# Banks of product tiles handed out by age across products; VectorE adds a group's first bank ahead of its split

## What is computed

```python
# block 1
r, k, v = (x_r @ w_r, x_k @ w_k, x_v @ w_v)       # 2048 x 2048 each
y = recurrence(r, k, v, ...) @ w_o                # 2048 x 2048
x = x + gate * rms(y)
u = causal_dwconv(norm(x) @ ffn_w_in)             # 2048 x 11008
f = (silu(gate_half(u)) * value_half(u)) @ ffn_w_out   # 5504 x 2048
x = x + gate * rms(f)
# block 2
p = rms(x) @ w_in_2                               # 2048 x 5376
x = x + rms(concat(attention(p), hgrn2(p)) @ w_out_2)  # 2048 x 2048
h = rms(x) @ w_up_2                               # 2048 x 8192
x = x + rms(relu(h)**2 @ w_down_2)                # 8192 x 2048
```

## Time and profile before

| | us |
|---|---|
| runs of the kernel before | 3032.55, 3021.90, 3033.14 |
| their median | 3032.55 |
| the profiled execution | 3020.16 |
| its span in the profile | 3018.2 |

### The profile page before, as it was taken

One profiled execution on the slowest core, in us unless ns is written; L12 is line 12 of the kernel. 1 busy time (PEld: TensorE's weight loads), 2 busy tenths in 40 slices (PEclk: granted clock), 3 DMA queues, 4 the chain that ended last, 5 costly groups with the idle time before them and its releaser, 6 DMA issues.

```text
span 3018.2 us, 45825 instructions
## 1 busy us (share of the span) xinstructions
PE 2813.4 (93%) x19618; PEld 2380.1 (79%) x19618; DVE 1869.0 (62%) x2460; ACT 1283.6 (43%) x1735; POOL 100.8 (3%) x127
## 2 busy tenths in 40 slices
PE   6999986898988899999989999999999999999997
PEld 2487875777877688788878878888978888888886
DVE  3776745676655577657757656566657556566554
ACT  1243423333214655445425545456555444343443
POOL 0101101111000000000000000000000000000000
PEclk9999997898889999999999999999999999999999
DMA  9766642232216266666665554443444555555552
GB/s 380 252 237 205 209 167 67 85 111 78 79 64 212 95 226 193 223 212 207 224 194 182 183 180 131 165 145 106 132 146 165 192 186 187 173 191 182 169 194 84
DMA packets 289212, 514.11 MB, mean 170 GB/s; under 512 B 10097, under 2 KB 122737, under 8 KB 288881
## 3 DMA queue, kind: packets, MB, share of 16 engines
q1 hardware_dynamic: 286016, 500.21, 49.4%
q0 software_dynamic: 2560, 7.90, 0.8%
q10 hardware_dynamic: 432, 3.07, 0.3%
HBM read 508.91 MB, written 2.10 MB: 169 GB/s over the span
## 4 chain that ended last, share of the span: by engine, by line
PE 81%; DVE 8%; ACT 5%; issue 3%; DMA 2%; POOL 0%; DVEq 0%; SPq 0%; ACTq 0%
PE ps L767 43%; PE ps L769 21%; PE ps L733 2%; PE ps L906 1%; DMA RAWa<-in_ada_w 1%; PE ps L901 1%; DVE WLb L1702 1%; ACT WHb L1195 1%; PE ps L676 1%; PE ps L891 1%; PE ps L794 1%; PE ps L868 1%; PE ps L858 1%; PE ps L788 1%; PE ps L957 1%
## 5 line engine op out<-in xcount | busy, mean ns | idle before, releaser
L767 PE MATMUL ps<-XB,WHb 128*128 128x512 f32 x2304 | 831.6, 404 | 30.1 <-DVE WLb L1702 19.2
L769 PE MATMUL ps<-XB,WLb 128*128 128x256 f32 x2304 | 646.8, 281 | 0.0
L1702 DVE TENSOR_TENSOR WLb<-RAWb,WHb 128x2048 fp32r<-128x2048 f32 (+1 forms) x196 | 426.2, 2191 | 315.5 <-ACT WHb L1195 315.3
L767 PEld LDWEIGHTS ps<-XB,WHb 128*128 128x128 f32 x2304 | 437.4, 190 | 138.2 <-issue 24.5
L1702 DVE TENSOR_TENSOR WLd<-RAWd,WHd 128x2048 fp32r<-128x2048 f32 x144 | 328.6, 2290 | 325.6 <-ACT WHd L1195 325.6
L1195 ACT ACTIVATE WHb<-RAWb 128x2048 fp32r<-128x2048 f32 (+1 forms) x196 | 356.8, 1832 | 332.4 <-PE ps L769 330.5
L767 PE MATMUL ps<-XD,WHd 128*128 128x512 f32 x1280 | 461.9, 403 | 4.1 <-DVE R L1754 3.2
L769 PEld LDWEIGHTS ps<-XB,WLb 128*128 128x128 f32 x2304 | 439.3, 191 | 1.2
L1195 ACT ACTIVATE WHd<-RAWd 128x2048 fp32r<-128x2048 f32 x144 | 274.8, 1915 | 364.9 <-PE ps L769 364.9
L767 PE MATMUL ps<-FB,WHd 128*128 128x512 f32 x1024 | 364.8, 400 | 2.7 <-DVE UM L2309 2.7
L769 PE MATMUL ps<-XD,WLd 128*128 128x256 f32 x1280 | 361.0, 282 | 0.0
(11 more groups left out here) (329 smaller groups left out, 3518.6 us busy)
## 6 DMA issues: line engine op xcount, KB each, us to landing
RAWb<-in_ffn_w_in SPq DMA_DIRECT2D x168, 512.0 KB, 5.1
RAWd<-in_w_up SPq DMA_DIRECT2D x64, 1024.0 KB, 5.2
RAWd<-in_w_down SPq DMA_DIRECT2D x64, 1024.0 KB, 5.1
RAWa<-in_ada_w SPq DMA_DIRECT2D x48, 1024.0 KB, 7.4
RAWa<-in_rwkv_w_rkv SPq DMA_DIRECT2D x48, 1024.0 KB, 5.8
RAWb<-in_ffn_w_out SPq DMA_DIRECT2D x36, 1024.0 KB, 5.2
RAWs<-in_ada_w SPq DMA_DIRECT2D x32, 1024.0 KB, 5.1
RAWb<-in_w_in SPq DMA_DIRECT2D x44, 512.0 KB, 4.8
```

The source lines that it names most:

```text
L767: pe.matmul(bank[:, :], WH[tag][:, w, o:o + P], acts(k), start=(k == 0), stop=False)
L769: mm = pe.matmul(bank[:, 0:T], WL[tag][:, w, o:o + P], acts(k)[:, 0:T], start=False, stop=last)
L1702: dve.tensor_tensor(WL[tag][:, n % WN, 0:size], RAW[tag][:, slot, 0:size], WH[tag][:, n % WN, 0:size].bitcast(F32), ALU.subtract).then_inc ...
```

## The change

Two edits. The banks are handed out from a list in order of age: a tile takes the bank that has been handed out longest ago (among the first five in `g_r`, the first six in `g_p`), and the list goes on from product to product. It begins again at banks 0 to 6 in order at `g_r`, `g_o`, the first product of `g_f`, `g_p` and `g_o2`. And in the products that accumulate, VectorE adds the first tile of a group ahead of `walk`, so ahead of the split of chunk n + 2, and the other tiles behind it as before. ScalarE's and TensorE's code stay as they are, apart from the bank numbers.

```diff
         tile_bank, tile_before, in_bank = [], [], {}
+        by_age = []
         for gm in [g_r, g_k, g_v, g_o] + [x for p in g_f for x in p] + [g_p, g_o2] + [x for p in g_m for x in p]:
+            if gm in (g_r, g_o, g_f[0][0], g_p, g_o2):
+                by_age = list(range(7))
             for i in range(gm.tile0, gm.tile_end):
-                b = (i - gm.tile0) % {g_p: 6, g_r: 5}.get(gm, 7)
+                b = next(b for b in by_age if b < {g_p: 6, g_r: 5}.get(gm, 7))
+                by_age.remove(b)
+                by_age.append(b)
                 tile_bank.append(b)
                 tile_before.append(in_bank.get(b))
                 in_bank[b] = i
@@ vector_program: gemm
                         last = ch is chunks[-1]
+                        if last and evac is accumulate:
+                            accumulate(gm, g, 0, 1)
                         if last and g in evac_first:
                             evac(gm, g)
                         walk(min(ch["number"] + 2, limit - 1))
                         if hook:
                             hook(g, ci)
-                        if last and g not in evac_first:
+                        if last and evac is accumulate:
+                            accumulate(gm, g, 1, n_tiles(gm, g))
+                        elif last and g not in evac_first:
                             evac(gm, g)
@@
-            def accumulate(gm, g):
-                for t in range(n_tiles(gm, g)):
+            def accumulate(gm, g, first, end):
+                for t in range(first, end):
                     i, d = gm.base[g] + t, to_r(gm, g, t)
                     dve.wait_ge(s_tile, i + 1)
                     dve.tensor_tensor(d, banks[tile_bank[i]][:, 0:T], d, ALU.add).then_inc(s_acc, 1)
```

## The result

| | us |
|---|---|
| changed kernel, four runs | 2991.95, 2983.63, 2987.64, 2987.84 |
| its median | 2987.74 |
| kernel before, four runs | 3032.55, 3021.90, 3033.14, 3018.68, median 3027.23 |
| ratio | 0.9872, 95% interval 0.9839 to 0.9904 |
| spans of the profiled executions, before and after | 3018.2 and 2990.0 |

The change makes the kernel 1.3% faster. The forecast was a gain of 32.1 us, subtracted from a median of 3032.55, which with more runs turned out to be 3027.2. The forecast time of 3000.5 is 12.8 us above the measured median. Of these, 5.3 us are the base that was too high, and 7.4 us are gain: the medians of this set lie 39.5 us apart, 7.4 more than forecast.

A forecast was written before the change was run, and what follows sets the result against it. TensorE, busy 93% of the span, was taken to lose time to bank waits and its lower clock; 2.1 + 1.7 + 13.8 + 6.6 + 6.3 + 1.9 - 0.3 = 32.1 us off 3032.55 gave 3000.5, range 2984 to 3013.

The forecast's parts named there:

- 18 bank waits: At product starts and groups' fourth tiles, 31.7 us together: 16 were to go, those in g_k and g_v to shrink.
- 13.8 + 6.6 us: Ten waits at product starts gone, 13.8 us; six at fourth tiles in two short-chunk products gone, 6.6 us.
- 2.1 + 1.7 us: Waits at the starts of g_k and g_v shrink to 3.97 and 3.56 us, moving to the fourth tile.
- The restart: TensorE's slower first matmuls after a wait: 0.12 us at each of 16 waits, 1.9 us gained.
- The second chunk of a product, costed at nothing: After the restart in g_k, the second chunk's split was to end well ahead of its turn, costing nothing.
- The clock: Lower clock behind three waits goes with them, 6.3 us gained; the falls in g_k and g_v were left in.
- the clock rival: The clock stays up in g_k and g_v too: 4.7 us more gain, 2996 us, chance 20%.
- Edit 2 outside the short chunks: VectorE's early first tile brings nothing in g_m, and the later split is costed at nothing in mid-product.
- cover: In accumulating groups the moved split of chunk n + 2 still ends 3.4 us before TensorE needs the chunk.

The follow-up runs named there:

- both_again: The changed kernel run once more with no edit: median 2992.23 us of four runs, ratio 0.9891 to the kernel before.
- banks_by_age_alone: The changed kernel without VectorE's early first tile, only the list by age: median 3003.18 us, ratio 0.9925 to the kernel before.
- all_tiles_ahead: The changed kernel, but VectorE adds all four tiles of an accumulating group ahead of the split: median 2988.42 us, ratio 0.9879 to the kernel before.
- split_done_twice: all_tiles_ahead with the split behind an accumulating group made twice, same values: median 3010.68 us, ratio 0.9944 to the kernel before.
- early_tile_alone: The changed kernel without the list by age, every product beginning at bank 0: median 3026.59 us, ratio 0.9998 to the kernel before.
- columns_filled: The changed kernel with a 128-column matmul of constants ahead of each one-column product of the modulation vectors: one run, 2998.03 us.

## Why the prediction was right

**The places.** Of the 18 bank waits that the prediction named as movable, 16 are gone and two are left, at the fourth tiles of g_k and g_v. The list alone and the early tile alone show which edit took which.

**The size of the idle time.** The prediction had 13.8 + 6.6 us gone in sixteen waits and 2.1 + 1.7 us off the two others, 24.2 us. Measured are 34.5 - 10.1 = 24.4 us, less the new 0.7 us. In g_k the wait became 3.48 us (3.97 forecast), in g_v 3.91 (3.56 forecast). In g_k the restart came at 242.21, forecast 242.26, but TensorE was ready at 238.73, forecast 238.29: the eviction hangs on the other two engines and kept its time, and TensorE's own time differs by some tenths between executions. In both_again both waits were 3.9 us. The restart was taken as 0.12 us; the start behind 242.21 is 0.46 us later in place of 0.354, which is 0.11 us more.

**The second chunk of a product, costed at nothing.** This was wrong by 0.7 us in g_k: the third chunk's low part was late (the row at 253.39), since VectorE makes activations first. TensorE was ready for that chunk at 252.72, and the kernel before began it at 256.64, so 3.9 us later, of which some 2.4 us were its lower clock. In both_again, where the clock fell behind this wait as well, no wait on WLa came. I had looked at the second chunk's split only, and the one behind it was the one to check.

**The clock.** 6.3 us were forecast to come back at three places, and the two in g_k and g_v were left in. At all three it came back whole (PEclk 1.00 at 1216.50, 1540.10 and 2603). In g_k the clock did not fall behind the wait in this execution either, which was the clock rival, worth 2.4 us there, and in g_v the fall was 0.6 us smaller; that makes 9.3 us. The prediction did not reckon with falls that come elsewhere. Behind the narrow products of the third pair there is a new one, (1 - 0.72) x 6 = 1.7 us. Behind those of the second pair (1292) there is another, PEclk 0.77, so 1.4 us. Behind those of g_k PEclk is 0.51, against 0.72 in the kernel before (281.10 to 287.10), 1.3 us more:

```profile
278.00:284.00 6.00, 6.00 (x24) 0.51 1.01 373
1292.00:1298.00 6.00, 6.00 (x33) 0.77 1.00 308
```

Over the whole execution the mean granted clock is 0.958 before and 0.960 after. By the unrounded record of the traces, the lower clock took at most 125.5 us of the one and 118.6 of the other, 6.9 us less. That this is near 6.3 is luck: gains and losses that the forecast did not have cancel in this execution. In both_again the clock did fall behind the wait in g_k, so the rival held in one of two executions there and in neither in g_v.

One sentence of the prediction misread its rows: TensorE did not come back at the 1.2 GHz level behind the waits at 1223.57 and 2626.20. There the first matmul lasts 0.47 us, as at the 2.4 GHz level; the clock fell only after the restart.

**Edit 2 outside the short chunks.** The prediction said it brings nothing in g_m and costs nothing there. That it brings nothing is seen in banks_by_age_alone, which has no bank wait in g_m; that it costs nothing in all_tiles_ahead and split_done_twice, with a cover of 3.6 us where 3.4 were worked out. The Trainium skill's rule in "TensorE: Matmul & The Clock Gate", section "Architectural detail: the array is 16× 32×32, not 1× 128×128", that VectorE takes its instructions first in, first out, is what early_tile_alone shows as a price: two tiles held behind the split made waits of 3.79 us out of 1.59.

**What the prediction missed.** That edit 2 alone is worth nothing was not in it, though the sum held the reason. And the time itself was set on a median of three runs, two of them above all but one of the 25 later runs of the kernel before. The base was 5.3 us too high, and the gain 7.4 us short by the first set and about right by the second.

## What to carry to other kernels

Where a ring of buffers is started anew for each stage, look at the first items of the next stage: they wait on the newest buffers while older ones lie free, and handing them out by age across stages costs no instruction. Then only one item of a group is urgent. Serve that one ahead of long work in the queue and leave the others behind it, and work out how long that long work can be put off before it becomes the next wait.

## What the runs showed of the hardware that was not expected

**Two paces of the same matmuls.** At the 2.4 GHz level, a chunk of sixteen pairs takes either 5.54 or 5.66 us, and a product keeps one of the two paces for one or several groups. Both are seen in the same product of the same program in two executions. ScalarE's conversions follow TensorE chunk by chunk and show it. The changed kernel, first profile:

```profile
1579.11 1.92 ACT L1200 ACTIVATE WHb<-RAWb 128x2048 fp32r<-128x2048 f32 x1 [1.80 <-PE ps L774]
1584.77 1.92 ACT L1200 ACTIVATE WHb<-RAWb 128x2048 fp32r<-128x2048 f32 x1 [3.74 <-PE ps L774]
```

The same kernel, second profile (both_again):

```profile
1572.25 1.92 ACT L1200 ACTIVATE WHb<-RAWb 128x2048 fp32r<-128x2048 f32 x1 [1.60 <-PE ps L774]
1577.79 1.92 ACT L1200 ACTIVATE WHb<-RAWb 128x2048 fp32r<-128x2048 f32 x1 [3.63 <-PE ps L774]
```

The starts are 5.66 and 5.54 us apart. Worked out from the starts of TensorE's matmuls, a whole group at the quicker pace is 0.42 us shorter; 14 groups ran so in the first profile of the changed kernel, 23 in the second and 21 in the profile of before. Nine groups are 3.8 of the 11.5 us between the two executions of one program. The lower clock took at most 118.6 us of the first and 115.5 of the second, so it may be another 3.1 us; the rest is not accounted for. Seven groups are 2.9 us by which the first pair of profiles makes the gain look smaller. In the last feed-forward every group of every profile ran at the slower pace. What chooses the pace is not known; no run was made for it.

**Clock falls without a wait for a bank.** Eight narrow products, sixteen short instructions of one column in 1.95 us, stand behind a wait for VectorE's sum in g_k, in g_v and in the third pair's first product. In g_k, behind 1.3 to 1.4 us of idle time, a fall to 1.2 GHz for some microseconds followed in nine of the ten profiles, that of columns_filled among them. In the third pair's first product, behind 1.2 to 1.4 us, it followed in eight of the nine profiles in which nothing was put in. In g_v it came in all ten, but there the idle time ahead is 3.51 us, and in some profiles the clock was down before the narrow products began (at 414.7 in the changed kernel, whose narrow products start at 415.03). So waits and narrow products stand together at these places, and no run here parts them.
